# Six rows of x for the second half loaded and normed two units earlier in a hybrid block kernel

## The chip, the cores and the metric

The kernel runs on one core of a Trainium2 chip. The metric is the time of one execution on the device, in microseconds (us). TensorE is called PE in the profile, VectorE DVE, ScalarE ACT, GpSimd POOL, and SyncE SP. SP issues the kernel's DMAs, each in the order of its program.

## What is computed

The block normalises x (2048 positions of 1024 channels) row by row, projects it once, and feeds two branches. One is a short convolution with a gated linear recurrence, the other a gated causal convolution of width 31 over 512 channels. Both are normed, joined and projected, and a SwiGLU layer follows. The part that the change touches is this:

```python
def rmsnorm(x, g):
    xf = x.astype(jnp.float32)
    y = xf * lax.rsqrt(jnp.mean(xf * xf, axis=-1, keepdims=True) + EPS)
    return (y * g.astype(jnp.float32)).astype(x.dtype)
...
        h = rmsnorm(x, norm_mix[l])
        proj = jnp.einsum('bsd,de->bse', h, w_in[l])
...
        glu = v_cm * jax.nn.sigmoid(g_cm)
        d = causal_depthwise_conv(glu, dw31_w[l], dw31_b[l])
```

All is float32. The kernel splits each operand of a matmul into a high and a low part, and makes three matmuls of each product.

## The kernel before

The 2048 positions are two halves of 1024. A row of x in this text is a tile of 128 positions by 1024 channels, so each half has eight rows: 0 to 7, and 8 to 15. Each half is worked through in four units of 128 channels, so there are eight units, u = 0 to 7. A unit has two pairs of products on PE, pairs 2u and 2u + 1. Unit 3 is the last of the first half, and while its second pair (pair 7) runs, the normed rows of the second half begin to replace those of the first in h_hi and h_lo.

A row passes four engines. SP loads it into a buffer xt (`load_x`). ACT sums its squares and takes the root (`x_std`, L996 and L997), and DVE takes the reciprocal and scales the row (`x_norm`, L1460 and L1463). Then PE turns it into two PSUM banks (`turn_x`, L1912), ACT writes its high part (`x_hi`, L1007), and DVE its low part (`x_lo`, L1471). There are only these two banks for it, so a row is turned only when the low part of the row before it is written. Rows 8 to 11 are turned at four places in pair 7, and rows 12 to 15 at four places in the first half of pair 8:

```python
        TURN_FIRST = {(1, 0, 0): 0, (1, 0, 4): 1, (1, 1, 0): 2, (1, 1, 4): 3}
...
        TURN_REST = {(0, 0, 1): 4, (0, 0, 5): 5, (0, 1, 1): 6, (0, 1, 5): 7}
```

In every unit DVE works off the convolution of width 31 as 31 operations over 1024 positions (`conv31`, L1623 for the first and L1629 for the others), each adding one tap to a sum in the PSUM tensor acc. Other work of DVE is put between the taps at written-out places: a place is the number of the tap ahead of which it stands. The recurrence of the unit before (`scan`, L1555) stands at place 22. Before, all eight x_norm and x_lo stand in unit 3. POOL does the element-wise work of the recurrence (L776 to L805), the low parts of the weights (`split_lo`, L740) and of c (L834), the gate product glu (L763), and at the end of a unit `output(u - 1)` (L746), which waits for scan(u - 1). ACT's `gates(u)` waits for scan(u - 1) too. Each engine works off its own program in order. The gate product of a unit has a buffer for every other unit, so DVE may be nearly a unit late without holding PE up, except through what PE waits for by itself, such as x_lo.

Of the kernel before, what the change touches and what calls it, by code (L numbers as in the profile page):

```python
# [18 lines left out]
F32 = mybir.dt.float32  # L19
# [3 lines left out]
P = 128  # L23
TILE = 512
KIB = 1024
# [5 lines left out]
def hybrid_block(nc, x, norm_mix, w_in, conv4_w, conv4_b, gate_a_w, gate_a_b, gate_x_w, gate_x_b,  # L31
                 lru_lambda, dw31_w, dw31_b, cm_ln_g, cm_ln_b, out_norm_lru, out_norm_cm,
                 w_out, norm_ffn, w_gate, w_up, w_down, norm_final, out):
    S, D = x.shape[1], x.shape[2]
    CH = conv4_b.shape[1]
    NJ = CH // P
# [7 lines left out]
    NT = S // P  # L44
    TPH = HALF // P
# [31 lines left out]
    with ExitStack() as ctx:  # L77
        base = (nc.sbuf_base + 63) // 64 * 64

        def at(name, shape, dt, offset):  # L80
            return nc.alloc_sbuf_tensor_at(name, shape, dt, offset=base + offset)
# [57 lines left out]
        y_hi = [at(f"y_hi{n}", [P, KD, P], F32R, o * KIB) for n, o in enumerate((104, 120, 152, 160))]  # L139
        y_lo = [at(f"y_lo{n}", [P, KD, P], F32R, o * KIB) for n, o in enumerate((96, 124, 156, 164))]  # L140

        xt = [at(f"xt{s}", [P, D], F32, o * KIB) for s, o in enumerate((168, 172, 176, 160, 164))]
        gw_raw = at("gw_raw", [P, NJ, 2, P], F32, 180 * KIB)
        xl = at("xl", [P, HALF + 32], F32, 184 * KIB)
        glu = [at(f"glu{s}", [P, HALF + 32], F32, 184 * KIB + 4224 * (1 + s)) for s in range(2)]
# [10 lines left out]
        o = 218 * KIB  # L156
# [183 lines left out]
        SCAN_AT, CENTRE_AT, LATE_AT = 22, 16, 27  # L340
        W_OUT_AT = (12, 14, 17, 19)
        CENTRE_AT_LAST, ROW0_AT = 16, 24
        X_NORM_AT = (7, 8, 9, 10, 12, 13, 14, 15)
        X_LO_AT = (9, 10, 11, 12, 14, 15, 16, 17)
        SCAN_AT_LAST = 11
        NORM_STEP = {2: 2, 3: 5}

# [16 lines left out]
        def summed_quarter(m, what):  # L364

            return 3 * m + {"11": 1, "12": 2, "22": 3}[what]

        def xb(g):
            return g if g < 5 else g - 5 if g < TPH else g % 3

        def x_loaded(g):
            b = xb(g)
            return (s_x[b], 16 * sum(xb(o) == b for o in range(g + 1))) if b < 3 else (s_xr[b - 1], 16)

        def aux_x(g):

# [29 lines left out]
        def _(sp_):  # L406
# [120 lines left out]
            for u in range(UNITS):  # L527
                if u == NJ - 1:

                    load_raw(2 * u + 4)  # L530
                    for g in range(TPH + 3, NT):
                        load_x(g)
                    load_raw(2 * u + 5)
                elif u == UNITS - 1:
                    sp_.wait_ge(s_pair[3], PPAIRS)
                    load_norm(1)
                    store_swish(0)
                    sp_.wait_ge(s_yswst[0], 16)
                    load_y(0)
                else:  # L540
                    load_raw(2 * u + 4)
                    load_raw(2 * u + 5)
                if u == NJ - 2:
                    for g in range(TPH, TPH + 3):
                        load_x(g)
                if u >= 1:
                    store_d(u - 1)
                    store_y(u - 1)
                if u == NJ:
                    units_stored(NJ)  # L550
                    sp_.wait_ge(s_aux_done[1], aux_x(NT - 1) + 1)
                    load_norm(0)
# [425 lines left out]
        def _(act):  # L978
# [15 lines left out]
            def x_std(g):  # L994
                act.wait_ge(*x_loaded(g))
                step(a.activation(junk[:, :], xt[xb(g)][:, :], ACT.Square, accum_out=ssq[:, g:g + 1]))  # L996
                a.activation(rstd[:, g:g + 1], ssq[:, g:g + 1], ACT.Sqrt, bias=eps[:, 0:1], scale=1.0 / D).then_inc(s_std, 1)  # L997
# [157 lines left out]
            for u in range(UNITS):  # L1155
                evacuate(u, 0, True)
                evacuate(u, 1, True)
                if 2 * u + 2 < PPAIRS:
                    split_hi(2 * u + 2)
                if u >= 1:  # L1160
                    gates(u - 1)
                    gate_functions(u - 1)
                if u == NJ - 1:
                    for g in range(TPH, TPH + 3):
                        x_std(g)
                if u == N0 + 2:
                    norm_swish(0)
                evacuate(u, 0, False)
                if u == NJ - 1:

                    x_hi(TPH)
                    x_std(TPH + 3)
                    x_hi(TPH + 1)
                    x_std(TPH + 4)
                    x_hi(TPH + 2)
                    x_hi(TPH + 3)
                    x_std(TPH + 5)
                if u >= 1:
                    two_minus(u - 1)
                evacuate(u, 1, False)  # L1180
                short_product(u, 3)
                if u == NJ - 1:
                    x_hi(TPH + 4)
                    x_std(TPH + 6)
                if u == NJ - 1:
                    x_hi(TPH + 5)
                    x_std(TPH + 7)
                    x_hi(TPH + 6)
                if u >= 1:
                    root(u - 1)  # L1190
                if u == NJ - 1:
                    x_hi(TPH + 7)
                if 2 * u + 3 < PPAIRS:
                    split_hi(2 * u + 3)
                c_split(u)
                if u == N0:
                    squares_lru(0)
                    squares_cm(0)
                if u == N0 + 1:
                    norm_std(0, 7)  # L1200
                    norm_rms_lru(0, 6)
                if u == N0 + 2:
                    norm_rms_cm(0, 6)
# [244 lines left out]
        def _(dve):  # L1448
# [122 lines left out]
            def add_row(w, between=None):  # L1571

                if w == 4:
                    norm_rms(1)
                if w % 4 == 0:
                    dve.wait_ge(s_rms, w // 4 + 1)
                dve.wait_ge(s_xr[w % 4], 16 * (w // 4 + 1 + (w % 4 >= 2)))
                line = row[w % 4]
                for group in range(2):
                    if group and between:  # L1580
                        between()
                    for dh in range(2):
                        e = 2 * group + dh
                        cols = slice(dh * TILE, (dh + 1) * TILE)
                        dve.wait_ge(s_out[e], w + 1)
                        if group:
                            dve.wait_ge(s_outf[dh], w + 1)
                        v.scalar_tensor_tensor(out=line[:, cols], in0=ps[e],
                                               scalar=rms[:, 2 * w + group:2 * w + group + 1],
                                               in1=line[:, cols], op0=ALU.mult, op1=ALU.add).then_inc(s_outf[e], 1)  # L1590

            def conv31(u):
                j = u % NJ
                t = glu[u % 2]
                last = 0
                for k in range(TAPS31):
                    place = k
                    if u == NJ - 1:

                        for g in range(TPH):  # L1600
                            if place == X_NORM_AT[g]:
                                x_norm(TPH + g)
                            if place == X_LO_AT[g]:
                                x_lo(TPH + g)
                    if place == CENTRE_AT and u == N0:
                        norm_centre(0, 6)
                    if u >= 1 and place == (SCAN_AT_LAST if u == UNITS - 1 else SCAN_AT):
                        scan(u - 1)
                    if u == UNITS - 1 and place == ROW0_AT:
                        norm_rms(0)  # L1610
                        add_row(0)
                    if u == UNITS - 1 and place == CENTRE_AT_LAST:
                        norm_centre(1, 6)
                    if u == UNITS - 1 and place in W_OUT_AT:
                        w_out_lo(W_OUT_AT.index(place))
                    if place == LATE_AT:
                        if u == N0 + 1:
                            norm_scale(0)
                    if k == 0:
                        dve.wait_ge(s_glu, (NS + 1) * (u + 1))  # L1620
                        if u >= 1:
                            dve.wait_ge(s_conv31, u)
                        ins = v.tensor_scalar(acc[:, :], t[:, 0:HALF], col(j, R_DW), col(j, R_DWB), ALU.mult, ALU.add)  # L1623
                    else:
                        dve.wait_ge(s_dve, last)
                        if k == TAPS31 - 1 and u >= 2:
                            dve.wait_ge(s_dst[u % 2], 16 * (u // 2))
                        into = dst[u % 2] if k == TAPS31 - 1 else acc
                        ins = v.scalar_tensor_tensor(out=into[:, :], in0=t[:, k:k + HALF], scalar=col(j, R_DW + k),  # L1629
                                                     in1=acc[:, :], op0=ALU.mult, op1=ALU.add)  # L1630
                    if k == TAPS31 - 1:
                        ins.then_inc(s_conv31, 1)
                    else:
                        steps[0] += 1
                        last = steps[0]
                        ins.then_inc(s_dve, 1)
# [579 lines left out]
```

## Time and profile before

| | |
|---|---|
| runs of the kernel before | 1954.06 us median of 3 (1951.34 to 1956.23) |
| the profiled execution | 1952.01 us |
| its span in the trace | 1950.2 us |
| PE busy in the span | 1880.1 us, 96% |
| DVE busy | 1143.1 us, 59% of the span; 321.88 us of the 350 us from 50 to 400 us |
| mean granted clock of PE | 0.986 |

The trace gives every instruction with its start and its duration, and for an engine that sat idle what released it. DVE and ACT durations hold a tail that overlaps the next instruction, so the cost of one in a row of them is the distance between two starts. Times in rows count from the span's start.

### The profile page before, as it was taken

The numbers are of one execution on the slowest core, as the hardware profiler recorded it, in microseconds if no ns is written. First come the engines' busy times: TensorE is split into PE (matmuls) and PEld (weight loads), VectorE is DVE, ScalarE is ACT, GpSimd is POOL, SyncE is SP. The second block draws the span as 40 slices with busy tenths as digits, with TensorE's granted clock in tenths as the row PEclk, the third lists the DMA queues.
The fourth block names the chain that finished last, engine by engine and source line by source line (L and its number), as shares of the span: only waits on it lengthen the run. The fifth ranks groups of instructions, "written<-read, shape, count | busy, mean of one in ns | idle before, by whom it ended". The sixth has DMA issues, their size and how long they took to land. (4 is left out here: it accounts for less than half of the span.)

```text
span 1950.2 us, 22241 instructions
## 1 busy us (share of the span) xinstructions
PE 1880.1 (96%) x8338; PEld 1549.9 (79%) x8338; DVE 1143.1 (59%) x1089; ACT 813.5 (42%) x936; POOL 1151.6 (59%) x427
## 2 busy tenths in 40 slices
PE   6999899987999999999999899999999999999997
PEld 5888688765888788888888688888888788888886
DVE  6899899989555845455454744544543224433446
ACT  6456855674563533233333532333333232222234
POOL 2477486955642567666655655555555766776663
PEclk9999999988999999999999999999999999999999
DMA  6123223144859453344334623332342755555455
GB/s 190 44 59 104 76 67 106 65 140 145 289 169 291 132 144 121 124 135 145 108 124 142 225 87 102 107 108 86 102 134 103 293 219 194 195 194 211 168 185 214
DMA packets 242335, 284.97 MB, mean 146 GB/s; under 512 B 12078, under 2 KB 167726, under 8 KB 241754
## 3 DMA queue, kind: packets, MB, share of 16 engines
q1 hardware_dynamic: 242266, 284.04, 44.0%
q8 instruction: 45, 0.74, 0.2%
q14 instruction: 24, 0.20, 0.0%
HBM read 201.68 MB, written 82.31 MB: 146 GB/s over the span
## 5 line engine op out<-in xcount | busy, mean ns | idle before, releaser
L856 POOL TENSOR_TENSOR t_lo<-t_sum,t_hi 128x2048 fp32r<-128x2048 f32 x44 | 206.6, 4696 | 167.9 <-ACT t_hi L1267 167.9
L1629 DVE SCALAR_TENSOR_TENSOR acc<-glu,par,acc 128x1024 f32<-128x1024 f32 x232 | 299.0, 1289 | 7.2
L850 POOL TENSOR_TENSOR b_lo<-m_raw,b_hi 128x1536 fp32r<-128x1536 f32 x44 | 157.0, 3568 | 182.1 <-ACT b_hi L1262 119.9
L939 POOL TENSOR_TENSOR f_lo<-f_raw,f_hi 128x2048 fp32r<-128x2048 f32 (+1 forms) x42 | 181.7, 4326 | 131.0 <-ACT f_hi L1407 131.0
L1887 PE MATMUL ps<-h_hi,w_hi 128*128 128x512 f32 x512 | 202.1, 395 | 2.6 <-POOL w_lo L740 2.6
L1888 PE MATMUL ps<-h_lo,w_hi 128*128 128x512 f32 x512 | 200.3, 391 | 0.0
L1889 PE MATMUL ps<-h_hi,w_lo 128*128 128x512 f32 x512 | 200.2, 391 | 0.0
L1668 DVE TENSOR_TENSOR t_sum<-m_raw 128x512 f32<-128x512 f32 x88 | 140.6, 1618 | 98.9 <-PE acc L1889 90.7
L1407 ACT CAST f_hi<-f_raw 128x2048 fp32r<-128x2048 f32 (+1 forms) x42 | 74.3, 1768 | 267.9 <-PE ps L1889 177.8
L1887 PE MATMUL ps<-wd_hi,f_hi 128*128 128x512 f32 x462 | 180.7, 391 | 3.1 <-POOL wd_lo L946 3.1
L1889 PE MATMUL ps<-wd_hi,f_lo 128*128 128x512 f32 x462 | 180.7, 391 | 0.0
L1888 PE MATMUL ps<-wd_lo,f_hi 128*128 128x512 f32 x462 | 180.5, 391 | 0.0
L1838 DVE TENSOR_TENSOR wd_raw<-wd_raw 128x1024 f32<-128x1024 f32 (+1 forms) x30 | 69.8, 2328 | 177.2 <-DMA wd_raw<-in_w_down 177.2
L1887 PE MATMUL ps<-a_hi,t_hi 128*128 128x512 f32 x440 | 171.6, 390 | 0.8 <-DVE p5s L1731 0.8
L1888 PE MATMUL ps<-a_lo,t_hi 128*128 128x512 f32 x440 | 171.4, 390 | 0.0
L1889 PE MATMUL ps<-a_hi,t_lo 128*128 128x512 f32 x440 | 171.4, 389 | 0.0
L1887 PE MATMUL ps<-wo_hi,y_hi 128*128 128x512 f32 x256 | 106.5, 416 | 11.2 <-DVE wo_lo L1566 11.2
L1887 PEld LDWEIGHTS ps<-h_hi,w_hi 128*128 128x128 f32 x512 | 96.9, 189 | 23.0 <-POOL w_lo L740 3.0
L1889 PEld LDWEIGHTS ps<-h_hi,w_lo 128*128 128x128 f32 x512 | 96.6, 189 | 20.3
L1888 PEld LDWEIGHTS ps<-h_lo,w_hi 128*128 128x128 f32 x512 | 96.6, 189 | 19.6 <-issue 0.2
L1887 PE MATMUL acc<-a_hi,t_hi 128*128 128x512 f32 x264 | 103.9, 394 | 7.3 <-DVE gt L1715 5.0
L1887 PE MATMUL ps<-a_hi,b_hi 128*128 128x512 f32 x264 | 103.4, 392 | 2.6 <-DVE a_lo L1644 2.6
(214 smaller groups left out, 4517.4 us busy)
## 6 DMA issues: line engine op xcount, KB each, us to landing
f_raw<-f_scr SPq DMA_DIRECT2D x35, 1024.0 KB, 4.9
wd_raw<-in_w_down SPq DMA_DIRECT2D x60, 512.0 KB, 6.6
f_scr<-fs SPq DMA_DIRECT2D x110, 256.0 KB, 2.1
m_raw<-in_w_gate SPq DMA_DIRECT2D x88, 256.0 KB, 4.0
m_raw<-in_w_up SPq DMA_DIRECT2D x88, 256.0 KB, 5.0
w_raw<-in_w_in SPq DMA_DIRECT2D x32, 512.0 KB, 5.4
f_scr<-gt SPq DMA_DIRECT2D x44, 256.0 KB, 2.0
xt<-in_x SPq DMA_DIRECT2D x16, 512.0 KB, 6.1
```

Of the source, the lines that this page charges most:

```text
L850: g.tensor_tensor(b_lo[b][:, :, :, :], m_raw[b][:, 0:3], f32(b_hi[b][:, :, :, :]), ALU.subtract).then_inc(s_mlo, 1)
L856: g.tensor_tensor(t_lo[b][:, :, :, :], t_sum[b][:, :, :, :], f32(t_hi[b][:, :, :, :]), ALU.subtract).then_inc(s_mlo, 1)
L939: g.tensor_tensor(f_lo[j % 3][:, 0:n], f_raw[j % 2][:, 0:n], f32(f_hi[j % 3][:, 0:n]), ALU.subtract).then_inc(s_dlo, 1)
L1407: a.copy(f_hi[j % 3][:, 0:n], f_raw[j % 2][:, 0:n]).then_inc(s_dhi, 1)
L1629: ins = v.scalar_tensor_tensor(out=into[:, :], in0=t[:, k:k + HALF], scalar=col(j, R_DW + k), in1=acc[:, :], op0=ALU.mult, op1=ALU.add)
L1668: v.tensor_tensor(into, in0, in1, ALU.subtract).then_inc(s_t, 1)
L1838: v.tensor_tensor(raw[:, 0, 0:c1 - c0], raw[:, 0, 0:c1 - c0], raw[:, 1, 0:c1 - c0], WD[m][2]).then_inc(s_t, 1)
L1887: pe.matmul(bank, lhs[0](c), rhs[0](c), start=first, stop=False, skip_group_check=more)
L1888: pe.matmul(bank, lhs[0](c), rhs[1](c), start=False, stop=False, skip_group_check=more)
L1889: mm = pe.matmul(bank, lhs[1](c), rhs[0](c), start=False, stop=last, skip_group_check=more)
```

## The change

Rows 8 to 13 are loaded in unit 0, behind the weights of pair 5, into xt0 to xt2 and three new buffers xt5 to xt7; rows 14 and 15 go to xt0 and xt1 as soon as rows 8 and 9 are turned. ACT's `x_std` for rows 8 to 10 stands in unit 1 and that for rows 11 to 13 in unit 2, between `gate_functions` and the evacuation of the unit's second pair. DVE's `x_norm` for them stands at the places 14, 16 and 18 of the units 1 and 2; rows 14 and 15 stay in unit 3, at places 13 and 15. The places of x_lo in unit 3 are spread from 9, 10, 11, 12, 14, 15, 16, 17 to 9, 11, 12, 14, 16, 17, 19, 21. The places of PE's `turn_x` are as before. The number of instructions is the same.

```diff
--- before.py
+++ after.py
@@ -139,7 +139,7 @@
         y_hi = [at(f"y_hi{n}", [P, KD, P], F32R, o * KIB) for n, o in enumerate((104, 120, 152, 160))]
         y_lo = [at(f"y_lo{n}", [P, KD, P], F32R, o * KIB) for n, o in enumerate((96, 124, 156, 164))]
 
-        xt = [at(f"xt{s}", [P, D], F32, o * KIB) for s, o in enumerate((168, 172, 176, 160, 164))]
+        xt = [at(f"xt{s}", [P, D], F32, o * KIB) for s, o in enumerate((168, 172, 176, 160, 164, 200, 208, 212))]
         gw_raw = at("gw_raw", [P, NJ, 2, P], F32, 180 * KIB)
         xl = at("xl", [P, HALF + 32], F32, 184 * KIB)
         glu = [at(f"glu{s}", [P, HALF + 32], F32, 184 * KIB + 4224 * (1 + s)) for s in range(2)]
@@ -340,8 +340,8 @@
         SCAN_AT, CENTRE_AT, LATE_AT = 22, 16, 27
         W_OUT_AT = (12, 14, 17, 19)
         CENTRE_AT_LAST, ROW0_AT = 16, 24
-        X_NORM_AT = (7, 8, 9, 10, 12, 13, 14, 15)
-        X_LO_AT = (9, 10, 11, 12, 14, 15, 16, 17)
+        X_NORM_AT = ((1, 14), (1, 16), (1, 18), (2, 14), (2, 16), (2, 18), (NJ - 1, 13), (NJ - 1, 15))
+        X_LO_AT = (9, 11, 12, 14, 16, 17, 19, 21)
         SCAN_AT_LAST = 11
         NORM_STEP = {2: 2, 3: 5}
 
@@ -365,12 +365,15 @@
 
             return 3 * m + {"11": 1, "12": 2, "22": 3}[what]
 
+        XB = (0, 1, 2, 3, 4, 0, 1, 2, 0, 1, 2, 5, 6, 7, 0, 1)
+        s_row = [*s_x, s_xr[2], s_xr[3], s_xr[2], s_xr[3], s_xr[0]]
+
         def xb(g):
-            return g if g < 5 else g - 5 if g < TPH else g % 3
+            return XB[g]
 
         def x_loaded(g):
-            b = xb(g)
-            return (s_x[b], 16 * sum(xb(o) == b for o in range(g + 1))) if b < 3 else (s_xr[b - 1], 16)
+            done = s_row[xb(g)]
+            return done, 16 * sum(s_row[xb(o)] is done for o in range(g + 1))
 
         def aux_x(g):
 
@@ -528,7 +531,7 @@
                 if u == NJ - 1:
 
                     load_raw(2 * u + 4)
-                    for g in range(TPH + 3, NT):
+                    for g in range(TPH + 6, NT):
                         load_x(g)
                     load_raw(2 * u + 5)
                 elif u == UNITS - 1:
@@ -540,8 +543,9 @@
                 else:
                     load_raw(2 * u + 4)
                     load_raw(2 * u + 5)
-                if u == NJ - 2:
-                    for g in range(TPH, TPH + 3):
+                if u == 0:
+                    sp_.wait_ge(s_part, 1)
+                    for g in range(TPH, TPH + 6):
                         load_x(g)
                 if u >= 1:
                     store_d(u - 1)
@@ -1160,8 +1164,8 @@
                 if u >= 1:
                     gates(u - 1)
                     gate_functions(u - 1)
-                if u == NJ - 1:
-                    for g in range(TPH, TPH + 3):
+                if 1 <= u <= 2:
+                    for g in range(TPH + 3 * (u - 1), TPH + 3 * u):
                         x_std(g)
                 if u == N0 + 2:
                     norm_swish(0)
@@ -1169,22 +1173,18 @@
                 if u == NJ - 1:
 
                     x_hi(TPH)
-                    x_std(TPH + 3)
                     x_hi(TPH + 1)
-                    x_std(TPH + 4)
                     x_hi(TPH + 2)
+                    x_std(TPH + 6)
                     x_hi(TPH + 3)
-                    x_std(TPH + 5)
+                    x_std(TPH + 7)
                 if u >= 1:
                     two_minus(u - 1)
                 evacuate(u, 1, False)
                 short_product(u, 3)
                 if u == NJ - 1:
                     x_hi(TPH + 4)
-                    x_std(TPH + 6)
-                if u == NJ - 1:
                     x_hi(TPH + 5)
-                    x_std(TPH + 7)
                     x_hi(TPH + 6)
                 if u >= 1:
                     root(u - 1)
@@ -1574,7 +1574,7 @@
                     norm_rms(1)
                 if w % 4 == 0:
                     dve.wait_ge(s_rms, w // 4 + 1)
-                dve.wait_ge(s_xr[w % 4], 16 * (w // 4 + 1 + (w % 4 >= 2)))
+                dve.wait_ge(s_xr[w % 4], 16 * (w // 4 + 1 + (1, 0, 2, 2)[w % 4]))
                 line = row[w % 4]
                 for group in range(2):
                     if group and between:
@@ -1598,10 +1598,10 @@
                     if u == NJ - 1:
 
                         for g in range(TPH):
-                            if place == X_NORM_AT[g]:
-                                x_norm(TPH + g)
                             if place == X_LO_AT[g]:
                                 x_lo(TPH + g)
+                    if (u, place) in X_NORM_AT:
+                        x_norm(TPH + X_NORM_AT.index((u, place)))
                     if place == CENTRE_AT and u == N0:
                         norm_centre(0, 6)
                     if u >= 1 and place == (SCAN_AT_LAST if u == UNITS - 1 else SCAN_AT):
```

DVE's program in unit 1, the kernel before. L1623 is the first tap, an L1629 row is so many further taps, L1555 is scan(0), and L1559 keeps its last state:

```order
L1623 TENSOR_SCALAR acc<-glu_170,par 128x1024
L1629 SCALAR_TENSOR_TENSOR acc<-glu_170,par,acc 128x1024 x21
L1555 SCALAR_TENSOR_TENSOR cv_132<-uw,su 128x1024
L1559 COPY hl<-cv_132 128x1
L1629 SCALAR_TENSOR_TENSOR acc<-glu_170,par,acc 128x1024 x8
L1629 SCALAR_TENSOR_TENSOR dst_149<-glu_170,par,acc 128x1024
```

and in the changed kernel, where xt_162 to xt_164 are the buffers xt0 to xt2 that now hold the rows 8 to 10:

```order
L1623 TENSOR_SCALAR acc<-glu_173,par 128x1024
L1629 SCALAR_TENSOR_TENSOR acc<-glu_173,par,acc 128x1024 x13
L1460 RECIPROCAL rstd<-rstd 128x1
L1463 SCALAR_TENSOR_TENSOR xt_162<-xt_162,rstd,g_row 128x1024
L1629 SCALAR_TENSOR_TENSOR acc<-glu_173,par,acc 128x1024 x2
L1460 RECIPROCAL rstd<-rstd 128x1
L1463 SCALAR_TENSOR_TENSOR xt_163<-xt_163,rstd,g_row 128x1024
L1629 SCALAR_TENSOR_TENSOR acc<-glu_173,par,acc 128x1024 x2
L1460 RECIPROCAL rstd<-rstd 128x1
L1463 SCALAR_TENSOR_TENSOR xt_164<-xt_164,rstd,g_row 128x1024
L1629 SCALAR_TENSOR_TENSOR acc<-glu_173,par,acc 128x1024 x4
L1555 SCALAR_TENSOR_TENSOR cv_132<-uw,su 128x1024
```

Three x_norm, each of a reciprocal and a scaling, now stand between the taps ahead of scan(0). Unit 2 has the same three ahead of scan(1), for rows 11 to 13.

DVE's program in unit 3, the kernel before, from the first tap on (L1471 is x_lo, two instructions of one row):

```order
L1623 TENSOR_SCALAR acc<-glu_170,par 128x1024
L1629 SCALAR_TENSOR_TENSOR acc<-glu_170,par,acc 128x1024 x6
L1460 RECIPROCAL rstd<-rstd 128x1
L1463 SCALAR_TENSOR_TENSOR xt_164<-xt_164,rstd,g_row 128x1024
L1629 SCALAR_TENSOR_TENSOR acc<-glu_170,par,acc 128x1024
L1460 RECIPROCAL rstd<-rstd 128x1
L1463 SCALAR_TENSOR_TENSOR xt_162<-xt_162,rstd,g_row 128x1024
L1629 SCALAR_TENSOR_TENSOR acc<-glu_170,par,acc 128x1024
L1471 TENSOR_TENSOR h_lo<-ps,h_hi 128x4x128 x2
```

and the changed kernel from the same tap on:

```order
L1623 TENSOR_SCALAR acc<-glu_173,par 128x1024
L1629 SCALAR_TENSOR_TENSOR acc<-glu_173,par,acc 128x1024 x8
L1471 TENSOR_TENSOR h_lo<-ps,h_hi 128x4x128 x2
L1629 SCALAR_TENSOR_TENSOR acc<-glu_173,par,acc 128x1024 x2
L1471 TENSOR_TENSOR h_lo<-ps,h_hi 128x4x128 x2
L1629 SCALAR_TENSOR_TENSOR acc<-glu_173,par,acc 128x1024
L1471 TENSOR_TENSOR h_lo<-ps,h_hi 128x4x128 x2
L1629 SCALAR_TENSOR_TENSOR acc<-glu_173,par,acc 128x1024
L1460 RECIPROCAL rstd<-rstd 128x1
L1463 SCALAR_TENSOR_TENSOR xt_162<-xt_162,rstd,g_row 128x1024
L1629 SCALAR_TENSOR_TENSOR acc<-glu_173,par,acc 128x1024
```

The first x_norm of the unit stood ahead of the first x_lo, three of them by place 9; now the first x_lo comes behind nine taps with no x_norm ahead of it in this unit.

## Rows read from the trace of the kernel before

**Rows 1.** The page: busy time, the chain that ended last, the loads of x (KB, median us to landing)

```profile
PE 1880.1 (96%) x8338; PEld 1549.9 (79%) x8338; DVE 1143.1 (59%) x1089; ACT 813.5 (42%) x936; POOL 1151.6 (59%) x427
...
PE 40%; DVE 1%; POOL 1%; issue 0%; DMA 0%; ACT 0%; POOLq 0%; SPq 0%; DVEq 0%; ACTq 0%
...
xt<-in_x SPq DMA_DIRECT2D x16, 512.0 KB, 6.1
```

**Rows 2.** PE's timeline, pairs 7 and 8: start, duration, idle before and its releaser

```profile
202.37 1.06 PE L1912 MATMUL ps<-ident,xt 128*128 128x128 f32 x8 [2.11 <-issue]
...
207.17 1.21 PE L1912 MATMUL ps<-ident,xt 128*128 128x128 f32 x8 [0.98 <-issue]
...
215.10 1.18 PE L1912 MATMUL ps<-ident,xt 128*128 128x128 f32 x8
...
227.62 1.67 PE L1912 MATMUL ps<-ident,xt 128*128 128x128 f32 x8 [4.29 <-issue]
```

**Rows 3.** Windows: us, busy of PE PEld DVE ACT POOL, granted PEclk, DMA

```profile
229.00:230.00 1.00, 1.00 (x5) 0.81 (x4) 0.03 (x1) 0.99 (x3) 0.97 (x1) 0.50 0.00 0
...
232.00:233.00 1.00, 1.00 (x5) 0.56 (x3) 1.00 (x2) 0.27 (x1) 0.00 (x0) 1.00 0.00 0
```

**Rows 4.** DVE's timeline, units 1 to 3

```profile
96.36 1.35 DVE L1623 TENSOR_SCALAR acc<-glu,par 128x1024 f32<-128x1024 f32 x1 [2.43 <-POOL gh L767]
97.74 27.79 DVE L1629 SCALAR_TENSOR_TENSOR acc<-glu,par,acc 128x1024 f32<-128x1024 f32 x21
126.33 2.29 DVE L1555 TENSOR_TENSOR_SCAN cv<-uw,su 128x1024 f32<-128x1024 f32 x1 [0.80 <-POOL su L805]
...
142.60 1.35 DVE L1623 TENSOR_SCALAR acc<-glu,par 128x1024 f32<-128x1024 f32 x1 [2.00 <-POOL gh L767]
...
188.84 1.35 DVE L1623 TENSOR_SCALAR acc<-glu,par 128x1024 f32<-128x1024 f32 x1 [2.00 <-POOL gh L767]
```

**Rows 5.** POOL's timeline, unit 1

```profile
109.53 2.40 POOL L786 TENSOR_TENSOR su<-su,uw 128x1024 f32<-128x1024 f32 x1 [1.44 <-ACT su L1124]
...
119.02 2.42 POOL L796 TENSOR_TENSOR cv<-cv,prod 128x1024 f32<-128x1024 f32 x1
...
126.48 4.35 POOL L834 TENSOR_TENSOR c_lo<-cv,c_hi 128x1024 fp32r<-128x1024 f32 x1 [0.18 <-ACT c_hi L1136]
```

**Rows 6.** ACT's timeline, units 1 and 3

```profile
113.25 0.58 ACT L1053 COPY xl<-ps 128x512 f32<-128x512 f32 x1 [3.80 <-PE ps L1889]
...
198.01 1.04 ACT L996 ACTIVATE junk<-xt 128x1024 bf16<-128x1024 f32 x1
...
203.39 0.57 ACT L1053 COPY xl<-ps 128x512 f32<-128x512 f32 x1
...
226.22 1.06 ACT L1007 CAST h_hi<-ps 128x512 fp32r<-128x512 f32 x2
```

**Rows 7.** DVE's timeline, x_norm in unit 3

```profile
200.78 0.16 DVE L1460 RECIPROCAL rstd<-rstd 128x1 f32<-128x1 f32 x1 [2.65 <-ACT rstd L997]
...
202.18 1.28 DVE L1629 SCALAR_TENSOR_TENSOR acc<-glu,par,acc 128x1024 f32<-128x1024 f32 x1
...
220.65 2.23 DVE L1463 SCALAR_TENSOR_TENSOR xt<-xt,rstd,g_row 128x1024 f32<-128x1024 f32 x1
```

**Rows 8.** POOL's timeline, the operations that DVE met

```profile
219.40 2.40 POOL L786 TENSOR_TENSOR su<-su,uw 128x1024 f32<-128x1024 f32 x1 [18.82 <-ACT su L1124]
...
339.69 2.40 POOL L834 TENSOR_TENSOR c_lo<-cv,c_hi 128x1024 fp32r<-128x1024 f32 x1
```

**Rows 9.** DVE's timeline, unit 5

```profile
329.73 2.29 DVE L1530 TENSOR_TENSOR nd<-nd,ps 128x2048 f32<-128x2048 f32 x1 [2.06 <-PE ps L1938]
...
339.75 4.49 DVE L1555 TENSOR_TENSOR_SCAN cv<-uw,hl,su 128x1024 f32<-128x1024 f32 x1
```

**Rows 10.** Lines of the trace to 620 us: busy us, mean ns of one, idle before

```profile
L740 POOL TENSOR_TENSOR w_lo<-w_raw,w_hi 128x2048 fp32r<-128x2048 f32 x15 | 73.3, 4885 | 19.1 <-ACT w_hi L992 19.1
...
L1471 DVE TENSOR_TENSOR h_lo<-ps,h_hi 128x512 fp32r<-128x512 f32 x32 | 20.7, 684 | 6.8 <-ACT h_hi L1007 6.8
```

## The prediction

> **What bounds the kernel now.** I read the page first: PE is busy for 96% of the span and holds the chain that ended last with 40% of the span against 1% for any other engine [rows 1], so a change counts only by what it does to PE's waits. PE's timeline around the turn to the second half shows the waits at issue: 2.11 us before row 8 is turned, 0.98 before row 9 and 4.29 before row 13, after which PE's clock is granted at 0.50 (1.2 GHz) for some 3.6 us and is back at 1.00 (2.4 GHz) by 232 [rows 2, 3]. Then DVE's timeline. It is the nearest to full: it enters the units 1 to 3 only 2.43, 2.00 and 2.00 us after the unit before, waiting for POOL's glu, and waits 0.80 for POOL ahead of scan(0) [rows 4]. That is all the slack that DVE has in a unit, and three x_norm now go into each of two units. ACT and POOL come next, since they share the work around each scan [rows 5, 6].
>
> **The change, part by part.**
>
> *Loads.* Six rows go out behind pair 5's weights in unit 0, before unit 1 begins at 96.36. A load lands 6.1 us after its issue in the median [rows 1], and the first x_norm stands at 114.9 (below). I cost them at nothing; the cover is over 10 us. Rows 14 and 15 wait for turns 8 and 9, which ends early enough as long as DVE is the later one.
>
> *ACT.* Three x_std took 198.01 to 203.39, 5.38 us, a table load among them [rows 6]. In unit 1 they stand ahead of an evacuation; ACT's next wait, 3.80 us before 113.25, takes up most of them, and about 1.2 us go on. But the operation of ACT ahead of this wait (two_minus), which POOL's L786 needs, moves by 5 us: L786 goes from 109.53 to about 114.4, where it ends at 116.8 [rows 5]. This puts POOL's work exactly beside DVE's new x_norm. In unit 3 the three x_std are gone from ahead of turn 8. That is the gain of the change: turns 8 and 9 could go 2.1 and 3.1 us earlier.
>
> *DVE, plain price.* From the reciprocal's start at 200.78 to the next tap at 202.18 an x_norm takes 1.40 us. A tap takes 27.79/21 = 1.32, some of it a wait for the tap ahead of it, which work in between hides, so I take 1.3 [rows 4, 7]. Six are 7.8 us. The two waits ahead of scans (0.80 each) and the two ahead of the units (2.00 each) take up 5.6, so by plain price DVE enters unit 3 only 2.2 us late.
>
> *DVE, price beside POOL.* The x_norm at 220.65 took 2.23 us instead of 1.28: POOL's operation ran until 219.40 + 2.40 = 221.80, and the x_norm ended 1.08 later [rows 7, 8]. The scan at 339.75 took 4.49 instead of 2.29: POOL's ran until 342.09, and the scan ended 2.15 later [rows 4, 8, 9]. The other way round, POOL's c_lo took 4.35 beside the scan at 126.33 [rows 4, 5]. So a DVE operation that reads two tensors in SBUF waits for the end of the POOL operation in progress, and POOL's next one for it. The taps, which read acc in PSUM, keep their 1.32. Now I walk along. Unit 1: place 14 comes at 96.36 + 1.38 + 13 x 1.32 = 114.9, the scaling is ready at 115.1, and L786 runs until 116.8: 1.7 us. Two taps on, the next is ready at 120.6, and the L796 of 119.02, now some 1.3 later, runs until 122.8: 2.1. The third meets the operation that this one held up, 2.1 again. The scan, ready near 135.1, meets a w_lo (L740, 4.6 us by its mean from [rows 10]) until 137.0: 1.9. In unit 2 I get 1.2, 2.1 and 1.9 the same way; the scan meets nobody, since POOL stands in L746, which waits for this scan. Seven meetings, 13.0 us. With the 2.2 of the plain price DVE enters unit 3 15.2 us late, at 204.0 instead of 188.84 [rows 4]. Queued behind scan(1) are also POOL's L746 and ACT's gates of unit 2, for which PE waits about 1 us.
>
> The Trainium skill, SBUF — State Buffer, section Who interferes with whom, says that a VectorE instruction with two SBUF inputs and a GpSimd instruction that reads SBUF exclude each other for the whole instruction. By that rule all seven meetings cost what is left of POOL's instruction, which comes to the 13.0 us; by the one row of an x_norm (0.95 us) six would cost 5.7, with a scan's 2.2 together 7.9, which would put turn 9 at 4 us late and the end at about 5, near 1959. The rule is what speaks most against this change, and no row here contradicts it.
>
> *PE in unit 3.* The first x_lo now stands behind nine taps: 204.0 + 1.38 + 8 x 1.32 = 215.9. Half of it (0.68 us [rows 10]) frees the first bank, so turn 9 goes near 216.5 instead of 207.17, 9.3 us later [rows 2]. PE is ready for it near 205, as a step of one turn and twelve matmuls takes 207.17 - 202.37 - 0.98 = 3.8 us and turn 8 is at 202.37 - 2.11 = 200.3 and the 1 us for the gates. The wait is 11 us. After the 4.29 us wait the halved clock cost about 3.6 x 0.47 = 1.7 us [rows 2, 3], and I add the same here: turns 10 and 11 are then 10 to 11 us late, and I take 10, since DVE's x_lo and ACT have caught up some of it there. The wait before turn 13 stays: x_hi(12) stood 226.22 - 215.10 = 11.1 us behind turn 11, with an x_std between in both programs [rows 2, 6]. It keeps its length and its clock loss, and all is 10 us late. Spreading x_lo costs nothing of its own, since DVE waits there for ACT.
>
> *After unit 3.* DVE has six x_norm fewer in unit 3 (8.4 us) and catches up. In unit 5 it waits 2.06 us for PE even before [rows 9]; it will wait longer there. From then on DVE and POOL follow PE, and no later stretch gives PE's 10 us back or adds to them. So the sum is +10 us on the profiled 1952.0. That execution is 2.05 us below the median of the runs shown, 1954.06, and against that median I forecast 1964.
>
> **Bounds.** The meetings cost nothing at least, and at most a whole POOL operation each: five at 2.4 and two at 4.6 make 21 us, 8 more than I take. I take the walk, since most of its terms come out near the upper end of 2.4 by themselves: DVE held up by POOL is lined up with POOL's next start. Turn 9's lateness is DVE's less 5.9 us (15.2 gave 9.3), so that is the point from which the change loses. The clock term is 0 to 2.5 us.
>
> **Rivals.** (A) The new x_norm don't meet POOL, or don't wait for it: DVE is 2.2 us late, turns 8 to 11 run at 3.65 to 3.8 us a step from 200.3, turn 11 is at 211.3 instead of 215.10, and the wait before turn 13 moves along; with x_std(14) and (15) out of the way of x_hi another 1 or 2 us go: 5 us faster, 1949. For it speaks that only few of the 16 x_norm so far were stretched, against it that the others ran while POOL stood still. This is the case on the other side: it holds below 5.9 us of lateness. (B) Phases are kinder and half of the 13 us is paid: DVE is 8.7 late, turn 9 2.8 late, with the clock and the wait for gates 3 us slower in all, 1957. POOL's gaps of a microsecond or two around its waits speak for it. (C) The forecast, 7 to 13 us slower. (D) Each late unit pushes POOL's and ACT's chain so far that PE also waits for c's low part or for weights in the second half: a w_lo held up as the 4.35 us c_lo was costs 2 us each, three of them 6 more, 1970.
>
> **How the numbers follow.** C 0.60, B 0.18, D 0.14, A 0.08. A measurement here tells 0.3%, 5.9 us, from no change. A is faster by 5, of which I put half beyond the bound; B is within it; C lies mostly beyond it and D wholly: faster 0.04, same 0.22, slower 0.74. The range leaves out A and the far part of D: 1953 to 1970. C's own is 1961 to 1967.
>
> **What would show it.** Right: x_norm in units 1 and 2 of 2 to 3.3 us each, DVE's first tap of unit 3 near 204, turn 9 near 216 with a wait of 11 us for h_lo, a clock of 0.50 behind it, PE about 10 us late at 350 us. Wrong: x_norm at 1.28, the first tap of unit 3 before 195, no long wait at turn 9. A first tap near 204 with PE on time again at 350 us would mean that a later wait had room, which I found nowhere.

## Result: slower by 0.53%, and the profile after

The changed kernel takes 1963.18 us in the median of 5 runs (1959.85 to 1965.8), the kernel before 1953.95 in the median of 5 (1950.14 to 1956.23). The ratio is 1.0053, 95% interval 1.0039 to 1.0066. The forecast of 1964.0 and its direction held. The profiled execution took 1963.8 us, with a span of 1962.0 against 1950.2 before.

PE's busy time hardly moved. The page's rows answer to [rows 1]:

```profile
PE 1882.7 (96%) x8338; PEld 1551.4 (79%) x8338; DVE 1154.2 (59%) x1089; ACT 815.1 (42%) x937; POOL 1156.8 (59%) x427
...
xt<-in_x SPq DMA_DIRECT2D x16, 512.0 KB, 6.4
```

DVE is busy 11.1 us more for the same 1089 instructions. DVE's timeline shows the longer operations in the units 1 and 2, and what they do to the start of unit 3 (start, duration, operation, idle time before with its releaser; it answers to [rows 4, 7]):

```profile
96.84 1.35 DVE L1623 TENSOR_SCALAR acc<-glu,par 128x1024 f32<-128x1024 f32 x1 [2.43 <-POOL gh L771]
98.22 17.19 DVE L1629 SCALAR_TENSOR_TENSOR acc<-glu,par,acc 128x1024 f32<-128x1024 f32 x13
...
115.51 2.96 DVE L1463 SCALAR_TENSOR_TENSOR xt<-xt,rstd,g_row 128x1024 f32<-128x1024 f32 x1
118.39 2.60 DVE L1629 SCALAR_TENSOR_TENSOR acc<-glu,par,acc 128x1024 f32<-128x1024 f32 x2
...
121.09 3.21 DVE L1463 SCALAR_TENSOR_TENSOR xt<-xt,rstd,g_row 128x1024 f32<-128x1024 f32 x1
...
126.93 3.10 DVE L1463 SCALAR_TENSOR_TENSOR xt<-xt,rstd,g_row 128x1024 f32<-128x1024 f32 x1
...
135.11 3.90 DVE L1555 TENSOR_TENSOR_SCAN cv<-uw,su 128x1024 f32<-128x1024 f32 x1
...
151.10 1.35 DVE L1623 TENSOR_SCALAR acc<-glu,par 128x1024 f32<-128x1024 f32 x1
...
169.77 3.01 DVE L1463 SCALAR_TENSOR_TENSOR xt<-xt,rstd,g_row 128x1024 f32<-128x1024 f32 x1
...
189.12 2.30 DVE L1555 TENSOR_TENSOR_SCAN cv<-uw,su 128x1024 f32<-128x1024 f32 x1
...
203.51 1.35 DVE L1623 TENSOR_SCALAR acc<-glu,par 128x1024 f32<-128x1024 f32 x1
204.89 10.56 DVE L1629 SCALAR_TENSOR_TENSOR acc<-glu,par,acc 128x1024 f32<-128x1024 f32 x8
215.37 1.28 DVE L1471 TENSOR_TENSOR h_lo<-ps,h_hi 128x512 fp32r<-128x512 f32 x2
```

The first tap of unit 3 starts at 203.51 instead of 188.84, and the bracket that stood there before, a wait of 2.00 us, is gone: DVE is now the engine that is late. Each x_norm takes some 3 us, while the taps around it keep their 1.3. POOL's timeline of the same stretch says what the x_norm met (it answers to [rows 5]):

```profile
114.98 2.40 POOL L790 TENSOR_TENSOR su<-su,uw 128x1024 f32<-128x1024 f32 x1 [6.40 <-ACT su L1128]
118.07 2.67 POOL L797 TENSOR_TENSOR cv<-cv,prod 128x1024 f32<-128x1024 f32 x1 [0.68 <-ACT prod L1098]
120.81 2.41 POOL L800 TENSOR_TENSOR cv<-cv,prod 128x1024 f32<-128x1024 f32 x1
123.30 3.29 POOL L803 TENSOR_TENSOR cv<-cv,prod 128x1024 f32<-128x1024 f32 x1
126.55 2.40 POOL L809 TENSOR_TENSOR su<-su,cv 128x1024 f32<-128x1024 f32 x1
128.91 3.38 POOL L838 TENSOR_TENSOR c_lo<-cv,c_hi 128x1024 fp32r<-128x1024 f32 x1
132.25 4.61 POOL L744 TENSOR_TENSOR w_lo<-w_raw,w_hi 128x2048 fp32r<-128x2048 f32 x1
```

Read the two side by side. L790 ends at 114.98 + 2.40 = 117.38, and the x_norm of 115.51 ends at 118.47, 1.09 later. L800 ends at 123.22, the x_norm of 121.09 at 124.30, 1.08 later. L809 ends at 128.95, the third x_norm at 130.03, again 1.08 later. The scan of 135.11 ends at 139.01, 2.15 behind w_lo's 136.86. And POOL's operation behind each is stretched in its turn (L797 to 2.67, L803 to 3.29, c_lo to 3.38, against 2.4 alone), so POOL falls behind together with DVE, and the next x_norm finds an operation of POOL in progress again. PE's timeline shows the consequence (it answers to [rows 2]):

```profile
192.35 0.47 PE L1887 MATMUL ps<-c_hi,gw_hi 128*128 128x512 f32 x1 [0.46 <-ACT uw L1109]
...
201.31 1.03 PE L1912 MATMUL ps<-ident,xt 128*128 128x128 f32 x8
...
216.15 1.94 PE L1912 MATMUL ps<-ident,xt 128*128 128x128 f32 x8 [11.07 <-issue]
...
222.61 1.04 PE L1912 MATMUL ps<-ident,xt 128*128 128x128 f32 x8
...
226.22 1.04 PE L1912 MATMUL ps<-ident,xt 128*128 128x128 f32 x8
...
231.75 1.03 PE L1912 MATMUL ps<-ident,xt 128*128 128x128 f32 x8
...
238.65 1.67 PE L1912 MATMUL ps<-ident,xt 128*128 128x128 f32 x8 [3.13 <-issue]
```

These are the turns of rows 8 to 13. Row 8 goes without a wait, 1.06 us earlier than before (the 0.46 at 192.35 is the wait for ACT's gates). Row 9 then waits 11.07 us for the low part of row 8, which DVE writes from 215.37 on, and goes 8.98 us late. Row 11 is 11.12 late and row 13 is 11.03 late. The windows show the clock behind the wait (us, busy of PE PEld DVE ACT POOL, granted PEclk, DMA; they answer to [rows 3]):

```profile
216.00:217.00 1.00, 0.85 (x4) 0.88 (x5) 1.00 (x3) 0.00 (x0) 0.00 (x0) 0.50 0.00 0
...
221.00:222.00 1.00, 1.00 (x4) 0.81 (x3) 0.55 (x1) 0.00 (x0) 0.00 (x0) 0.50 0.00 0
222.00:223.00 1.00, 1.00 (x7) 0.79 (x7) 0.00 (x0) 0.00 (x0) 0.00 (x0) 0.95 0.00 0
```

PE works for some 6 us at 0.50 (1.2 GHz). One turn and its twelve matmuls take 222.61 - 216.15 = 6.46 us there, against 226.22 - 222.61 = 3.61 in the step behind it. Nothing later gives that back. In unit 5 DVE's L1530 waits for PE (it answers to [rows 9], where the wait was 2.06), and starts 10.75 us late:

```profile
340.48 2.29 DVE L1530 TENSOR_TENSOR nd<-nd,ps 128x2048 f32<-128x2048 f32 x1 [8.26 <-PE ps L1938]
```

### The profile page after: what moved, and what is told of

It is laid out like the page before. It is cut to its first block and busy times, and to the rows that moved or that the text cites. A ratio compares the mean times of both kernels' runs of the same rounds, so it can differ in the third digit from the quotient of the medians.

```text
span 1962.0 us, 22243 instructions
## 1 busy us (share of the span) xinstructions
PE 1882.7 (96%) x8338; PEld 1551.4 (79%) x8338; DVE 1154.2 (59%) x1089; ACT 815.1 (42%) x937; POOL 1156.8 (59%) x427
## 5 line engine op out<-in xcount | busy, mean ns | idle before, releaser
L1629 DVE SCALAR_TENSOR_TENSOR acc<-glu,par,acc 128x1024 f32<-128x1024 f32 x232 | 298.9, 1288 | 7.1
```

## Experiments

The theory is that an operation of DVE with two inputs in SBUF waits for the POOL operation in progress; six x_norm and a scan thereby make DVE some 15 us late, and PE pays for what of it exceeds 5.9 us at the first x_lo. The rivals are that the work added to DVE is the cost, whoever it meets; that the moved x_std or the moved loads are; or that the spread x_lo is. Diffs are against the changed kernel, `...` marks lines left out. Medians and ratios are against the kernel before on the same chip: 1953.9 us (35 runs) beside e1 to e4, 1953.29 (29) beside e5 to e8, and 1953.6 (15) beside e9. A ratio is not the quotient of the two medians, and near 1 the two can differ by 0.1%: e4_load, whose DVE works as before, has 1.0009 with equal medians. So a ratio of 1.001 is hardly told from no change here.

**e1_psum.** The same work at the same places, with one input of the six x_norm in PSUM. The gain row is left out of them, so the second half's values are not the reference's:

```diff
+                gain = acc if TPH <= g < TPH + 6 else g_row
-                                       in1=g_row[:, :], op0=ALU.mult, op1=ALU.mult).then_inc(s_xn, 1)
+                                       in1=gain[:, :], op0=ALU.mult, op1=ALU.mult).then_inc(s_xn, 1)
```

> The changed kernel, but the six early x_norm multiply by the PSUM tensor acc in place of the gain row in SBUF, so that each reads one tensor in SBUF; same size, same places, and the second half's values are not the reference's. If DVE pays for meeting POOL (theory), these six take 1.28 us each instead of 2.9 to 3.2, DVE's first tap of unit 3 comes near 195 instead of 203.5, with what is left of its lateness being 3.9 us of plain price per unit and a scan(1) that now meets a weight low part (up to 4 us); turn 9 goes near 207.5 with a wait of 3 us or less, and the kernel is 1 to 4 us slower than the kernel before, 7 to 10 us faster than the changed one. If it is the plain work in the units 1 and 2 that costs (rival: crowding), the first tap of unit 3 stays near 203 and the kernel 9 us slower.

Measured: 1953.6 us (12 runs), ratio 1.001 (1.0001 to 1.0019). DVE's timeline, and two operations of POOL's:

```profile
115.51 1.28 DVE L1464 SCALAR_TENSOR_TENSOR xt<-xt,rstd,acc 128x1024 f32<-128x1024 f32 x1
...
119.42 1.28 DVE L1464 SCALAR_TENSOR_TENSOR xt<-xt,rstd,acc 128x1024 f32<-128x1024 f32 x1
...
177.31 5.85 DVE L1556 TENSOR_TENSOR_SCAN cv<-uw,su 128x1024 f32<-128x1024 f32 x1
...
195.24 1.35 DVE L1624 TENSOR_SCALAR acc<-glu,par 128x1024 f32<-128x1024 f32 x1
```

```profile
114.99 2.42 POOL L790 TENSOR_TENSOR su<-su,uw 128x1024 f32<-128x1024 f32 x1 [6.40 <-ACT su L1128]
...
176.39 4.62 POOL L744 TENSOR_TENSOR w_lo<-w_raw,w_hi 128x2048 fp32r<-128x2048 f32 x1
```

The first x_norm starts at the very same 115.51, with L790 of POOL running, and takes 1.28 us. So do all six, and each of them starts while an operation of POOL is in progress. This is the experiment that decides: the operation, its size and its place are unchanged, and only where one input lies differs. Most of the loss is gone. But no gain appears either: DVE still enters unit 3 at 195.24. As the six x_norm no longer delay it, scan(1) comes at 177.31, beside the w_lo of 176.39, and takes 5.85 us; in the changed kernel it came at 189.12, met nobody and took 2.30.

**e2_gap.** The six x_norm earlier, where POOL stands waiting for ACT ahead of L790:

```diff
-        X_NORM_AT = ((1, 14), (1, 16), (1, 18), (2, 14), (2, 16), (2, 18), (NJ - 1, 13), (NJ - 1, 15))
+        X_NORM_AT = ((1, 9), (1, 10), (1, 11), (2, 9), (2, 10), (2, 11), (NJ - 1, 13), (NJ - 1, 15))
```

> The changed kernel with the x_norm of the rows 8 to 13 at the places 9, 10 and 11 of units 1 and 2, where POOL waits for ACT's two_minus, instead of 14, 16 and 18. Theory: the ones of unit 1 take 1.28 us, of unit 2 at most one meets POOL; scan(1), which comes later by the plain price, meets a weight low part (2 to 4 us). First tap of unit 3 near 195.5, turn 9 near 208, 1 to 5 us slower than the kernel before. Rival crowding: places within a unit don't matter, first tap near 203, 9 us slower.

Measured: 1954.62 us (11 runs), ratio 1.001 (1.0 to 1.002). Five of the six x_norm take 1.28 or 1.29 us and the last, at 162.28, takes 3.06. scan(1) meets POOL's w_lo as in e1_psum (4.36), DVE enters unit 3 at 196.14, and turn 9 waits 3.79 us. The same instructions in other places thus give back 0.4 of the 0.5%, and what is left is hardly told from no change.

**e3_std.** Loads and x_std as in the changed kernel, all eight x_norm and x_lo in unit 3 as before.

```diff
-        X_NORM_AT = ((1, 14), (1, 16), (1, 18), (2, 14), (2, 16), (2, 18), (NJ - 1, 13), (NJ - 1, 15))
-        X_LO_AT = (9, 11, 12, 14, 16, 17, 19, 21)
+        X_NORM_AT = ((NJ - 1, 7), (NJ - 1, 8), (NJ - 1, 9), (NJ - 1, 10), (NJ - 1, 12), (NJ - 1, 13), (NJ - 1, 14), (NJ - 1, 15))
+        X_LO_AT = (9, 10, 11, 12, 14, 15, 16, 17)
...
+                            if X_NORM_AT[g] == (u, place):
+                                x_norm(TPH + g)
                             if place == X_LO_AT[g]:
                                 x_lo(TPH + g)
-                    if (u, place) in X_NORM_AT:
-                        x_norm(TPH + X_NORM_AT.index((u, place)))
```

> The loads and the x_std of six rows early as in the changed kernel, but all x_norm and x_lo back at their old places in unit 3. Theory: DVE enters unit 3 within 2 us of before, PE's waits before turns 8 and 9 shrink from 3.1 us by at most 1 or 2 as the first x_norm still stands at place 7, and x_hi(12) comes less than 1 us earlier: 0 to 2 us faster than the kernel before. Rival, that the early x_std push ACT's and POOL's chain enough to cost by themselves: DVE enters unit 3 over 5 us late and the kernel is over 4 us slower.

Measured: 1952.31 us (11 runs), ratio 0.9995 (0.9985 to 1.0004). The moved x_std cost nothing that can be measured. But they delay POOL's chain, so that both scans come 0.03 us behind the start of POOL's c_lo and wait for it. In the kernel before, scan(0) came 0.15 us ahead of c_lo (126.33 against 126.48), took 2.29 us, and c_lo was the one that waited [rows 4, 5]. DVE's timeline of e3_std, and POOL's c_lo beside scan(0):

```profile
128.52 4.51 DVE L1555 TENSOR_TENSOR_SCAN cv<-uw,su 128x1024 f32<-128x1024 f32 x1 [1.83 <-POOL su L809]
...
174.77 4.51 DVE L1555 TENSOR_TENSOR_SCAN cv<-uw,su 128x1024 f32<-128x1024 f32 x1 [0.48 <-POOL su L809]
```

```profile
128.49 2.40 POOL L838 TENSOR_TENSOR c_lo<-cv,c_hi 128x1024 fp32r<-128x1024 f32 x1
```

**e4_load.** The loads and the buffers alone; x_std, x_norm and x_lo as before. The diff shows the first x_std; the others go back in the same way, and x_norm and x_lo as in e3_std.

```diff
-                if 1 <= u <= 2:
-                    for g in range(TPH + 3 * (u - 1), TPH + 3 * u):
+                if u == NJ - 1:
+                    for g in range(TPH, TPH + 3):
                         x_std(g)
...
```

> Only the loads and the buffers of the changed kernel; x_std, x_norm and x_lo of the kernel before. Theory: nothing waits for these loads but two x_std (0.4 and 0.9 us before), so within 2 us of the kernel before. If six loads in unit 0 hold up weights, PE would wait for w_lo in unit 1 or 2 and the kernel be slower.

Measured: 1953.8 us (12 runs), ratio 1.0009 (0.9998 to 1.0019). PE's waits are those of before, 2.11 before row 8 and 4.30 before row 13. No cost of the early loads can be measured. This execution enters unit 1 1.23 us later than the one before (DVE's first tap at 97.59 against 96.36), as do all with early loads, by 0.5 to 1.2 us. But in each of these traces the lag is there at the x_lo of 29.76 to 30.57 us (29.28 before), while the first early load is issued at 87.43 us in the changed kernel; so the loads are not its cause.

**e5_half.** The x_norm of unit 1 in POOL's gap, those of unit 2 as changed: half a dose.

```diff
-        X_NORM_AT = ((1, 14), (1, 16), (1, 18), (2, 14), (2, 16), (2, 18), (NJ - 1, 13), (NJ - 1, 15))
+        X_NORM_AT = ((1, 9), (1, 10), (1, 11), (2, 14), (2, 16), (2, 18), (NJ - 1, 13), (NJ - 1, 15))
```

> Half the dose: in unit 1 the x_norm stand at 9, 10 and 11, where POOL is idle, in unit 2 at 14, 16 and 18 as in the changed kernel. Theory: unit 1's three take 1.28 us, unit 2's near 3, first tap of unit 3 between that of the gap kernel (196.1) and of the changed one (203.5), near 198.5, turn 9 near 211, and the kernel 3 to 7 us slower than the kernel before. If only lateness of the scan mattered and not the x_norm's own meetings, it would be as the gap kernel, within 1 us.

Measured: 1957.37 us (12 runs), ratio 1.0023 (1.0012 to 1.0033). Two of unit 2's x_norm take 3.20 and 3.11 us, the first only 1.59, and scan(1) takes 3.90. DVE enters unit 3 at 197.70, and turn 9 goes at 210.34 after 5.63 us. The rival of the expectation, that it would be as e2_gap within 1 us, did not come true.

**e6_xlo.** The changed kernel with x_lo at its old places:

```diff
-        X_LO_AT = (9, 11, 12, 14, 16, 17, 19, 21)
+        X_LO_AT = (9, 10, 11, 12, 14, 15, 16, 17)
```

> The changed kernel with x_lo at its old places 9, 10, 11, 12, 14, 15, 16, 17; all else as changed. Theory: the spread of x_lo costs nothing, as DVE waits for ACT there: within 1.5 us of the changed kernel, 8 to 10 us slower than the kernel before, turn 9 near 216 again. Rival, that the spread holds PE up by itself: 4 us or more faster than the changed kernel.

Measured: 1965.08 us (6 runs), ratio 1.0061 (1.0045 to 1.0077); the interval overlaps with the changed kernel's. The median is 1.9 us above the changed kernel's and 11.8 above the kernel before's, a little more than the expected 1.5 and 10. Turn 9 goes at 216.83 after 11.05 us. So the spread x_lo is not where the loss comes from, and no gain or cost of it shows.

**e7_scan20.** All six x_norm in POOL's gaps, and scan(1) two places earlier:

```diff
-        X_NORM_AT = ((1, 14), (1, 16), (1, 18), (2, 14), (2, 16), (2, 18), (NJ - 1, 13), (NJ - 1, 15))
+        X_NORM_AT = ((1, 9), (1, 10), (1, 11), (2, 8), (2, 9), (2, 10), (NJ - 1, 13), (NJ - 1, 15))
...
-                    if u >= 1 and place == (SCAN_AT_LAST if u == UNITS - 1 else SCAN_AT):
+                    if u >= 1 and place == (SCAN_AT_LAST if u == UNITS - 1 else 20 if u == 2 else SCAN_AT):
```

> All six x_norm beside an idle POOL (9, 10, 11 in unit 1; 8, 9, 10 in unit 2), and scan(1) at place 20 instead of 22 of unit 2, so that it comes before POOL starts the weight low part. Theory: scan(1) takes at most 4 us instead of 4.4 but starts 2.6 us sooner, first tap of unit 3 near 193 to 194, turn 9 at or before 207, the kernel 0 to 3 us faster than the kernel before. If the scan's meeting is not what was left, as the gap kernel: 1 to 3 us slower than before.

Measured: 1950.12 us (12 runs), ratio 0.9985 (0.9975 to 0.9994), faster than both kernels. All six x_norm take 1.28 or 1.29 us. Its DVE and PE timelines:

```profile
155.22 1.29 DVE L1463 SCALAR_TENSOR_TENSOR xt<-xt,rstd,g_row 128x1024 f32<-128x1024 f32 x1
...
174.70 3.89 DVE L1555 TENSOR_TENSOR_SCAN cv<-uw,su 128x1024 f32<-128x1024 f32 x1
...
193.33 1.35 DVE L1623 TENSOR_SCALAR acc<-glu,par 128x1024 f32<-128x1024 f32 x1
```

```profile
205.97 1.21 PE L1912 MATMUL ps<-ident,xt 128*128 128x128 f32 x8 [1.63 <-issue]
...
225.93 1.94 PE L1912 MATMUL ps<-ident,xt 128*128 128x128 f32 x8 [3.12 <-issue]
```

**e8_best.** e7_scan20 with x_lo of rows 8 and 9 one place earlier, and row 12's x_hi ahead of an evacuation, to shorten the wait before turn 13. The diff leaves out the lines that it shares with e7_scan20:

```diff
...
-        X_LO_AT = (9, 11, 12, 14, 16, 17, 19, 21)
+        X_LO_AT = (8, 10, 12, 14, 16, 17, 19, 21)
...
+                if u == NJ - 1:
+                    x_hi(TPH + 4)
                 evacuate(u, 1, False)
                 short_product(u, 3)
                 if u == NJ - 1:
-                    x_hi(TPH + 4)
...
```

> As the kernel with scan(1) at place 20, and in unit 3 the first two x_lo one place earlier (8 and 10) and ACT's x_hi of row 12 ahead of the evacuation that it stood behind. Theory: the wait before turn 13 (3.1 us, an ACT queue wait) shrinks to 1 or 2 us and turn 9 comes near 205; 2 to 6 us faster than the kernel before. If moving x_hi only moves the wait on to turn 14, as the kernel with scan(1) at place 20.

Measured: 1950.35 us (12 runs), ratio 0.9985 (0.9974 to 0.9995), no better than e7_scan20. PE's timeline:

```profile
222.20 1.17 PE L1913 MATMUL ps<-ident,xt 128*128 128x128 f32 x8
228.59 1.44 PE L1913 MATMUL ps<-ident,xt 128*128 128x128 f32 x8 [2.47 <-issue]
```

Row 13 goes at 222.20 without a wait, and row 14 waits 2.47 us in its place: the wait has moved one turn on. The gain of 2 to 6 us that was expected over the kernel before did come (2.9 by the medians), but all of it was there in e7_scan20. The 2.49 us by which row 14 is ahead of e7_scan20 (231.08) don't show in the median, and that part stays unexplained.

**e9_lo_early.** The late DVE kept, and the first x_lo put near the start of the unit:

```diff
-        X_LO_AT = (9, 11, 12, 14, 16, 17, 19, 21)
+        X_LO_AT = (2, 4, 6, 8, 11, 14, 16, 18)
```

> The changed kernel, with x_lo at the places 2, 4, 6, 8, 11, 14, 16 and 18 of unit 3 instead of 9, 11, 12, 14, 16, 17, 19 and 21. The six early x_norm stay where they meet POOL, so DVE enters unit 3 as late as in the changed kernel, near 203.5. Theory (DVE's lateness costs only through the first x_lo, for which PE holds turn 9): the first x_lo stands behind two taps, turn 9 goes at about 203.5 + 1.35 + 1.3 + 0.7, near 207 instead of 216.15, after a wait of about 2 us instead of 11.07, and without the long idle stretch PE's clock stays at 1.00 there. Turn 11 comes near 217, some 2 us behind the kernel before, and the median near 1955 to 1956. Rival (the late DVE costs by itself, by POOL and ACT being pushed into the second half): turn 9 is early all the same, but the time stays above 1960. If x_lo were late for ACT's x_hi instead, x_lo would show waits for h_hi and the gain would be some 4 us of the 9.

Measured: 1954.62 us (11 runs), ratio 1.0012 (1.0002 to 1.0022). DVE and PE:

```profile
203.59 1.35 DVE L1623 TENSOR_SCALAR acc<-glu,par 128x1024 f32<-128x1024 f32 x1
...
206.16 1.28 DVE L1471 TENSOR_TENSOR h_lo<-ps,h_hi 128x512 fp32r<-128x512 f32 x2
```

```profile
206.95 1.21 PE L1912 MATMUL ps<-ident,xt 128*128 128x128 f32 x8 [1.79 <-issue]
...
214.48 1.10 PE L1912 MATMUL ps<-ident,xt 128*128 128x128 f32 x8
```

DVE is as late as in the changed kernel (203.59 against 203.51), all six x_norm are as long, and the loss is a quarter of what it was. So most of what the late DVE costs goes through the first x_lo. The expectation had turn 11 near 217 and the median at 1955 to 1956, both a little too late: turn 11 goes at 214.48, ahead of the 215.10 before. PE falls behind only at turn 15, 238.19 against 237.15, after a wait of 1.00 us; whether this is all that is left of the loss was not followed further.

## Why the prediction was right

**The chain from DVE to PE.** In every kernel with the first x_lo at place 9 and no x_norm ahead of it, turn 9 follows the first tap of unit 3 by the same distance (starts in us, off DVE's and PE's timelines; the last column is turn 9's start less the first tap's):

| | first tap, unit 3 | turn 9 | wait before it | ratio | distance |
|---|---|---|---|---|---|
| e7_scan20 | 193.33 | 205.97 | 1.63 | 0.9985 | 12.64 |
| e1_psum | 195.24 | 207.89 | 3.53 | 1.001 | 12.65 |
| e2_gap | 196.14 | 208.78 | 3.79 | 1.001 | 12.64 |
| e5_half | 197.70 | 210.34 | 5.63 | 1.0023 | 12.64 |
| changed | 203.51 | 216.15 | 11.07 | 1.0053 | 12.64 |
| e6_xlo | 204.20 | 216.83 | 11.05 | 1.0061 | 12.63 |

The forecast used 12.5. With turn 9 of before at 207.17, turn 9 is late from a first tap of 194.53 on, 5.7 us late; the forecast said 5.9. The times agree with it as far as they can tell: e7_scan20 (4.5 late) is faster than the kernel before, e1_psum (6.4) and e2_gap (7.3) are hardly told from it, e5_half (8.9) is slower. e9_lo_early shortens the distance to 3.36 and takes most of the cost away at the same lateness.

**Meetings with POOL.** Forecast: seven, 13.0 us. Measured: the six x_norm exceed 1.28 by 1.68, 1.93, 1.82, 1.73, 1.80 and 1.65, together 10.6, and scan(0) its 2.29 by 1.6: 12.2 us, with scan(1) free of a meeting, as the walk had it. The single terms were off by up to 0.5 (the first x_norm of unit 2 was put at 1.2 and took 1.73), partly against each other. e1_psum shows the cause, with 1.28 us against 2.93 to 3.21.

The Trainium skill, SBUF — State Buffer, section Who interferes with whom, says that two SBUF inputs are what make a VectorE instruction contend with a reading GpSimd instruction and that the one issued first blocks the other throughout. The traces agree: 1.28 us in e1_psum against 2.93 to 3.21 in the changed kernel, and stretched operations on both engines. No run here has a GpSimd operation that only writes.

**Plain price.** Forecast: 2.2 us late without the lock. In e7_scan20 DVE is 193.33 - 188.84 = 4.5 us late, of which 0.5 were there at unit 1 (96.83 against 96.36) and 1.9 are the two scans' excess (2.57 and 3.89 against 2.29). That leaves 2.1. (The scan stands two places earlier in this kernel, so it is not the changed kernel in all but the meetings.)

**Lateness of DVE.** Forecast 15.2, measured 14.7, of which 0.5 again were there at unit 1; the terms sum to 12.2 + 2.1 = 14.3, against the 14.2 that are left.

**The waits at the turns.** Turn 8 was put at 201.3, with 1 us for the gates, and came at 201.31. That it fits to 0.01 us is luck: the gates took only 0.46, and the rest is that this execution was 0.5 us behind already at unit 1. Turn 9 was put at 216.5 after 11 us and came at 216.15 after 11.07.

**Behind turn 9.** Here two terms were mis-sized, against each other. The clock was put at 1.7 us by the row of a shorter wait, with bounds of 0 to 2.5, and took 6.46 - 3.61 = 2.85 us, which is outside them. (The factor 0.47 in the forecast's 3.6 x 0.47 stands in no row; half the clock for 3.6 us would be 1.8.) The wait before turn 13 was said to keep its length and is 3.13 instead of 4.29 us; 0.96 us of the rest stands ahead of a matmul at 230.98. PE is 11.1 us late at turn 11 instead of 10, and L1530's start in unit 5 is 10.75 late. The medians differ by 9.2 us, with an interval of 7.6 to 12.9 (0.39 to 0.66% of 1954), so the lateness of this one execution fits them. That the forecast's 1964.0 came within 1 us of the median is partly luck, since both kernels' executions spread over 6 us. The forecast that nothing later adds was nearly right: the span of the profiled execution is 11.8 us longer, 1 us more than at L1530.

**The rivals.** Rival A, no lock and 5 us faster, can't be had by freeing the x_norm alone: e1_psum does that and is not faster (ratio 1.001). What A left out is that the x_std delay POOL, so that scans without the x_norm's delay meet it instead (e3_std: 4.51 twice; e1_psum: 5.85). Once both are attended to, e7_scan20 gains 0.15%, about 3 of A's 5 us. Rival B, half of the meetings, was put at 3 us slower in all with 2.8 us at turn 9; e5_half is that case, with turn 9 3.17 us late and 0.23%, 4.5 us. Rival D wanted 6 us of further waits for weights or c's low part; PE's waits for w_lo are 3.2 us against 2.6 before, those for c_lo 7.3 against 7.4.

## What to carry to other kernels

Work moved to an engine that has slack must also be free of what its neighbours do at that moment: six VectorE operations of 1.28 us took 2.93 to 3.21 each beside GpSimd, and 1.28 or 1.29 when they stood in GpSimd's gaps (e7_scan20) or read one input from PSUM (e1_psum). Before moving work ahead of a point, find what the late engine still owes the critical one behind that point; here the one operation was x_lo, and either keeping DVE at most 7.3 us late (e1_psum, e2_gap) or moving the first x_lo seven places forward (e9_lo_early) removed most of the loss. Only e7_scan20, with the gaps and an earlier scan, came out ahead of the kernel before; the gaps alone (e2_gap) did not, and the earlier scan alone was not tried.

## What was not expected of the hardware

The time that PE spends at the halved clock behind a wait does not follow the wait's length. Behind 11.07 us in the changed kernel the turn and its twelve matmuls took 6.46 us, behind 11.05 us in e6_xlo 222.12 - 216.83 = 5.29, and behind 5.63 us in e5_half 216.67 - 210.34 = 6.33. Behind 3.53 and 3.79 us in e1_psum and e2_gap they took 5.41 and 5.38, and behind 1.63 us in e7_scan20 3.86, with the granted clock at 1.00. The step at 2.4 GHz is 3.6. So a wait of 11 us cost 1.7 us on top in one kernel and 2.9 in another, and what decides between the two was not tried.
